# Latents' attention of a hybrid diffusion step: raw scores are moved out of the PSUM banks by ScalarE in thirds, maxima and shifts work on the moved copy, and value products run two pairs behind

## The reference

```python
def one_block(qblk):
    s = jnp.einsum('bqkgd,blkd->bkgql', qblk, k).astype(jnp.float32) * scale
    p = jax.nn.softmax(s, axis=-1).astype(v.dtype)
    return jnp.einsum('bkgql,blkd->bqkgd', p, v)
```

## Time and profile before

| what | us |
|---|---|
| median of 3 runs | 2715.31 |
| lowest and highest | 2712.28, 2717.53 |
| the profiled execution, its own time | 2714.14 |
| its span in the profile | 2712.3 |
| first scores of the latents to the last output copy of their attention | 326.99 to 701.76 |

### The profile page before, as it was taken

How to read it: one execution, slowest core, us unless ns; L and a number is a source line. 1 busy time by engine, 2 the same in 40 slices (tenths; PEclk the granted TensorE clock), 3 DMA queues, 4 the chain that set the end, 5 groups by cost and what they waited for, 6 DMA issues and landing times.

```text
span 2712.3 us, 37077 instructions
## 1 busy us (share of the span) xinstructions
PE 2565.8 (95%) x15039; PEld 1926.0 (71%) x15039; DVE 1645.7 (61%) x2459; ACT 1193.8 (44%) x1950; POOL 235.9 (9%) x259
## 2 busy tenths in 40 slices
PE   7999799999899999999999999997799999999994
PEld 3444499999788677575767888884577777777773
DVE  2555677777333345757566344556676776777774
ACT  3311334444333233434343333342576766666663
POOL 1111100000000000000001000000010110101012
PEclk8999899999899999999999999998899999999997
DMA  9310000000101200101012200525688897988887
GB/s 320 135 66 32 0 1 1 1 1 1 63 32 51 96 16 1 55 1 55 1 39 82 78 32 32 190 98 186 236 289 309 281 329 271 312 305 289 305 274 221
DMA packets 176603, 345.01 MB, mean 127 GB/s; under 512 B 9338, under 2 KB 37580, under 8 KB 176434
## 3 DMA queue, kind: packets, MB, share of 16 engines
q1 hardware_dynamic: 166396, 314.09, 32.6%
q0 software_dynamic: 9472, 28.32, 4.1%
q10 hardware_dynamic: 566, 0.24, 0.0%
HBM read 304.35 MB, written 38.27 MB: 126 GB/s over the span
## 4 chain that ended last, share of the span: by engine, by line
PE 63%; issue 22%; DMA 8%; DVE 5%; ACT 1%; POOL 0%; POOLq 0%; DVEq 0%; SPq 0%; ACTq 0%
PE ps L1004 16%; PE ps L228 8%; DMA ffn_scratch<-WK 6%; PE ps L1358 6%; PE ps L751 5%; PE ps L1310 5%; PE ps L779 4%; PE ps L1905 4%; DVE WK L848 2%; PE ps L1421 2%; PE ps L1404 1%; PE ps L1324 1%; PE ps L2448 1%; PE ps L1381 1%; PE ps L1931 1%
## 5 line engine op out<-in xcount | busy, mean ns | idle before, releaser
L2527 ACT ACTIVATE RWr<-R 128x1024 fp32r<-128x1024 f32 x384 | 377.8, 1055 | 71.9 <-PE ps L2448 69.3
L2622 DVE TENSOR_TENSOR W_low<-R,RWr 128x1024 fp32r<-128x1024 f32 x256 | 301.4, 1219 | 84.5 <-ACT RWr L2527 82.4
L2448 PE MATMUL ps<-RWr,R1r 128*128 128x512 f32 x1024 | 329.6, 396 | 6.0 <-DVE R1r L2610 4.3
L1004 PE MATMUL ps<-W_high,tile_high 128*128 128x512 f32 x640 | 251.2, 392 | 7.7 <-DVE W_low L1082 7.2
L1004 PE MATMUL ps<-W_low,tile_high 128*128 128x512 f32 x640 | 250.6, 392 | 0.0
L1004 PE MATMUL ps<-W_high,tile_low 128*128 128x512 f32 x640 | 250.5, 391 | 0.0
L228 PE MATMUL ps<-RW,R 128*128 128x512 f32 (+1 forms) x640 | 248.9, 542 | 0.0
L2448 PEld LDWEIGHTS ps<-RWr,R1r 128*128 128x128 f32 x1024 | 192.9, 188 | 58.2 <-issue 14.2
L228 PEld LDWEIGHTS ps<-RW,R 128*128 128x128 f32 x640 | 119.2, 191 | 105.4 <-issue 101.5
L1074 DVE TENSOR_TENSOR tile_low<-R,tile_high 128x1024 fp32r<-128x1024 f32 x80 | 97.9, 1223 | 156.9 <-ACT tile_high L1030 156.7
L2622 DVE TENSOR_TENSOR tile_high<-R,RWr 128x1024 fp32r<-128x1024 f32 x128 | 150.8, 1219 | 29.8 <-ACT RWr L2527 29.5
(11 more groups left out here) (346 smaller groups left out, 4638.1 us busy)
## 6 DMA issues: line engine op xcount, KB each, us to landing
R<-in_w_dram SPq DMA_DIRECT2D x96, 2048.0 KB, 13.3
RW<-in_w_in_dram SPq DMA_DIRECT2D x11, 1024.0 KB, 5.4
R<-in_w_mod_dram SPq DMA_DIRECT2D x5, 2048.0 KB, 12.8
RW<-in_w_in_dram SPq DMA_DIRECT2D x5, 2048.0 KB, 8.4
RW<-in_w_mod_dram SPq DMA_DIRECT2D x4, 2048.0 KB, 11.3
WK<-in_w_mod_dram SPq DMA_DIRECT2D x3, 2048.0 KB, 7.8
mix_scratch<-R SPq DMA_DIRECT2D x10, 512.0 KB, 2.6
R<-mix_scratch SPq DMA_DIRECT2D x10, 512.0 KB, 7.0
```

Of the source, the lines that this page charges most:

```text
L1004: i = pe.matmul(bank(m % 4), Tsplit[a][:, m % 2, k, :], Wsplit[b][:, k, :], start=(k == 0 and n == 0), stop=(k == KD - 1 and n == 2))
L2448: m = pe.matmul(bank(bank_of(e, i, j)), stat[a][:, k, :], w[b][:, k % 2, :], start=(k == 0 and z == 0), stop=(k == KD - 1 and z == 2))
L2527: act.activation(ring_high[n % RING], pair_raw[i][j][:, 2 * q:2 * q + 2, :], ACT.Copy).then_inc(S("weights_high"), 1)
L2622: dve.tensor_tensor(ring_low[n % RING], pair_raw[i][j][:, 2 * q:2 * q + 2, :], ring_high[n % RING].bitcast(F32), ALU.subtract).then_inc(S( ...
```

## The change

The raw scores leave PSUM by a plain copy. `keep_scores(u)` (ScalarE) copies banks 0 to 5 in three pieces of 1024 elements into `probs[u % 3]`, which now has three buffers in place of two (the third lies in the front of WK; the small tiles of the stage move to where the rotary tables lay). `scores_done` rises three times a turn, once for each third; `scores(u + 1)` waits for `scores_kept` in place of the shifted pieces. `top_of` reads the copy in SBUF, by thirds: three maxima over 4 blocks each and two of two tiles. `shift` reads the copy and adds in place. `shifts` has two buffers. The value products run two turns behind the scores. The diff, with the moved tile addresses left out:

```diff
-            def scores(u, half):
+            def scores(u):
...
                     if u and b % 4 == 0:
-                        pe.wait_ge(S("kept_by_dve"), CTX_K + 3 * (u - 1) + b // 4 + 1)
+                        pe.wait_ge(S("scores_kept"), 3 * (u - 1) + b // 4 + 1)
...
-                m.then_inc(S("scores_done"), 1)
+                    if b % 4 == 3:
+                        m.then_inc(S("scores_done"), 1)
...
-            for u in range(len(turns) + 2):
-                if u < len(turns):
-                    scores(u, 0)
-                    scores(u, 1)
-                if u >= 2:
-                    turn_rows(u - 2)
-                v = u - 1
-                if 0 <= v < len(turns):
-                    weigh_rows(v, 0, range(0, 8))
-                if u < len(turns):
+            N = len(turns)
+            for u in range(N + 3):
+                if u < N:
+                    scores(u)
+                v = u - 2
+                if 0 <= v < N:
+                    weigh_rows(v, 0, range(0, 10))
+                if u >= 3:
+                    turn_rows(u - 3)
+                if 0 <= v < N:
+                    weigh_rows(v, 0, range(10, 12))
+                    weigh_rows(v, 1, range(0, 4))
+                if u < N:
                     turn_max(u)
-                if 0 <= v < len(turns):
-                    weigh_rows(v, 0, range(8, 12))
-                    weigh_rows(v, 1, range(0, 3))
-                if u < len(turns):
+                if 0 <= v < N:
+                    weigh_rows(v, 1, range(4, 12))
+                if u < N:
                     spread_max(u)
-                if 0 <= v < len(turns):
-                    weigh_rows(v, 1, range(3, 12))
...
-            def top_of(u, half):
-                dve.wait_ge(S("scores_done"), CTX_K + 2 * u + half + 1)
-                o = half * 3 * BANK
-                ch(dve.tensor_reduce(top_halves[half], ps[:, o:o + 3 * BANK].rearrange("p (b n) -> p n b", n=2 * P), AX, ALU.max))
-                if half:
-                    dve.tensor_tensor(top_halves[1], top_halves[0], top_halves[1], ALU.max).then_inc(S("max_ready"), 1)
+            def top_of(u, third):
+                dve.wait_ge(S("scores_kept"), 3 * u + third + 1)
+                src = probs[u % 3][:, 4 * third:4 * third + 4, :].rearrange("p b n -> p n b")
+                ch(dve.tensor_reduce(tops[min(third, 1)], src, AX, ALU.max))
+                if third == 1:
+                    ch(dve.tensor_tensor(tops[0], tops[0], tops[1], ALU.max))
+                elif third == 2:
+                    dve.tensor_tensor(tops[1], tops[0], tops[1], ALU.max).then_inc(S("max_ready"), 1)
...
-            def shift(u):
-                dve.wait_ge(S("max_kept"), u + 1)
-                dve.wait_ge(S("values_weighed"), CTX_Q + max(0, u - 1))
-                for p_ in range(3):
-                    dve.tensor_tensor(pT[u % 2][:, 4 * p_:4 * p_ + 4, :], ps[:, p_ * 2 * BANK:(p_ + 1) * 2 * BANK].rearrange("p (b n) -> p b n", b=4),
-                                      shifts.unsqueeze(1).broadcast_to([P, 4, 2 * P]), ALU.add).then_inc(S("kept_by_dve"), 1)
+            def shift(u, p_):
+                if p_ == 0:
+                    dve.wait_ge(S("max_kept"), u + 1)
+                E = probs[u % 3][:, 4 * p_:4 * p_ + 4, :]
+                dve.tensor_tensor(E, E, shifts[u % 2].unsqueeze(1).broadcast_to([P, 4, 2 * P]), ALU.add).then_inc(S("kept_by_dve"), 1)
...
-            for u in range(len(turns) + 1):
-                if u < len(turns):
-                    top_of(u, 0)
-                    top_of(u, 1)
+            N = len(turns)
+            for u in range(N + 2):
+                if 1 <= u <= N:
+                    shift(u - 1, 0)
+                    shift(u - 1, 1)
+                if u < N:
+                    for third in range(3):
+                        top_of(u, third)
+                if 1 <= u <= N:
+                    shift(u - 1, 2)
+                if u < N:
                     negate(u)
-                    shift(u)
-                if u:
-                    invert(u - 1)
+                if u >= 2:
+                    invert(u - 2)
...
+            def keep_scores(u):
+                act.wait_ge(S("values_weighed"), CTX_Q + max(0, u - 2))
+                if u == 2:
+                    act.wait_ge(S("kept_by_dve"), CTX_K)
+                for third in range(3):
+                    act.wait_ge(S("scores_done"), CTX_K + 3 * u + third + 1)
+                    act.activation(probs[u % 3][:, 4 * third:4 * third + 4, :],
+                                   ps[:, third * 2 * BANK:(third + 1) * 2 * BANK].rearrange("p (b n) -> p b n", b=4), ACT.Copy).then_inc(S("scores_kept"), 1)
...
-            for u in range(len(turns) + 2):
-                if u >= 2:
-                    keep_columns(u - 2)
-                if u < len(turns):
-                    if u:
-                        act.wait_ge(S("kept_by_dve"), CTX_K + 3 * u)
-                    keep_max(u)
-                    for p_ in range(3):
-                        exps_of(u, p_)
-                if 1 <= u <= len(turns):
-                    keep_rows(u - 1)
-                    T, g, hp = turns[u - 1]
+            N = len(turns)
+            for u in range(N + 3):
+                if u < N:
+                    keep_scores(u)
+                if u >= 3:
+                    keep_columns(u - 3)
+                if 1 <= u <= N:
+                    for p_ in range(3):
+                        exps_of(u - 1, p_)
+                if u < N:
+                    keep_max(u)
+                if 2 <= u < N + 2:
+                    keep_rows(u - 2)
+                if u < N:
+                    T, g, hp = turns[u]
```

More of the change, by code:

```diff
@@ L246, in build_program @@
         vv = work(14 * HKV * VW).rearrange("p (b n) -> p b n", b=14)
+        cos_at = used[0]
         cos_t = work(T_LAT * 64).rearrange("p (t f) -> p t f", t=T_LAT)
@@ L659, in build_program @@
         turns = [(T, g, hp) for T in range(T_CTX, NT) for g in range(HKV) for hp in range(2)]
[L660 to L664, removed]
+        probs = pT + [WK[:, 0:12 * 2 * P].rearrange("p (b n) -> p b n", b=12)]
+        assert cos_at + 2048 <= WORK_N
+        out_rows, tops, shifts = [[WK[:, cos_at + (2 * i + n) * 2 * P:cos_at + (2 * i + n + 1) * 2 * P] for n in range(2)] for i in range(3)]
+        top_diag = WK[:, cos_at + 1536:cos_at + 1792].rearrange("p (a n) -> p a n", a=2)
+        minus = WK[:, cos_at + 1792:cos_at + 1792 + P]
         def sset(s):
@@ L682, in queries_read @@
             else:
-                eng.wait_ge(S("scores_done"), CTX_K + 2 * (turns.index((T, g, 1)) + 1))
+                eng.wait_ge(S("scores_done"), CTX_K + 3 * (turns.index((T, g, 1)) + 1))
         def tile_scores(pe, T, k):
@@ L736, in pe_attn @@
                 weigh(T_CTX - 1, 3, b)
-            def scores(u, half):
+            def scores(u):
                 T, g, hp = turns[u]
[L741 to L747, removed]
+                if hp == 0:
+                    pe.wait_ge(S(f"queries_staged{g}"), T + 1)
+                if u == 0:
+                    pe.wait_ge(S("kept_by_act"), CTX_K)
+                    pe.wait_ge(S("kept_by_dve"), CTX_K)
+                for b in range(NK_LAT):
                     if u and b % 4 == 0:
-                        pe.wait_ge(S("kept_by_dve"), CTX_K + 3 * (u - 1) + b // 4 + 1)
+                        pe.wait_ge(S("scores_kept"), 3 * (u - 1) + b // 4 + 1)
                     for n, (a, c_) in enumerate(((0, 0), (0, 1), (1, 0))):
@@ L785, in turn_rows @@
                 pe.wait_ge(S("kept_by_act"), CTX_K + u + 1)
-                pe.wait_ge(S("kept_by_dve"), CTX_K + 3 * min(u + 2, len(turns)))
+                pe.wait_ge(S("max_kept"), min(u + 3, len(turns)))
                 for a in range(2):
@@ L920, in keep_columns @@
                 act.activation(R2[:, o:o + 2 * P], ps[:, 6 * BANK + 2 * P:7 * BANK], ACT.Copy).then_inc(S("attn_kept"), 1)
+            def keep_scores(u):
[6 more added lines that the diff above has]
+                                   ps[:, third * 2 * BANK:(third + 1) * 2 * BANK].rearrange("p (b n) -> p b n", b=4), ACT.Copy).then_inc(S("scores_kept"), 1)
             def keep_max(u):
                 act.wait_ge(S("max_spread"), u + 2)
-                act.activation(shifts, bank(6, 2 * P), ACT.Copy).then_inc(S("max_kept"), 1)
+                if u >= 2:
+                    act.wait_ge(S("kept_by_dve"), CTX_K + 3 * (u - 1))
+                act.activation(shifts[u % 2], bank(6, 2 * P), ACT.Copy).then_inc(S("max_kept"), 1)
             def exps_of(u, p_):
                 act.wait_ge(S("kept_by_dve"), CTX_K + 3 * u + p_ + 1)
-                E = pT[u % 2][:, 4 * p_:4 * p_ + 4, :]
+                E = probs[u % 3][:, 4 * p_:4 * p_ + 4, :]
                 act.activation(E, E, ACT.Exp, scale=SCALE).then_inc(S("probs_ready"), 1)
```

11 lines of the change are left out of this document (5 added, 6 removed).

## The result

The change makes the kernel slower: a median of 2755.04 us (2753.47 to 2756.17, 4 runs) against 2716.36 us of before in the same comparison, a ratio of 1.0145 with a 95% interval of 1.0127 to 1.0162. The forecast was 2699.4 us, range 2694 to 2710. The profiled execution has a span of 2754.3 us.

What follows compares the result with a forecast made beforehand. The prediction took TensorE as the bound, with one stall per turn waiting for VectorE's maxima. Turns -18.0, fill -1.4 and drain +3.5 summed to -15.9 us, from 2715.31 to 2699.4 us, range 2694 to 2710.

Steps and rivals of the forecast that it cites:

- turns of 10.62: Steady turns 2 to 31: each falls from 11.22 to 10.62 us, saving 18.0 us over 30 turns.
- The stall of 0.65: TensorE's transposes of the maxima start 0.65 us late each turn, waiting for VectorE; removing this saves 0.60 a turn.
- TensorE's own idle of 0.37: Steady turns: the lower bound on time removed per turn, 0.37 us, from TensorE's own idle; 0.60 was taken instead.
- The step that failed: VectorE's reduction of 1024 elements from the SBUF copy, priced between two measured rows at 1.22 us.
- The overlap margin: VectorE in a steady turn: maxima ready 0.5 us before TensorE asks, third shift piece and `negate` done 0.4 before.
- the ring's own sum: Steady turn's cycle from spreading through `keep_max`, shifts, maxima and `negate` to spreading: 10.25 us against TensorE's 10.62.
- slow strides: Rival: strided SBUF reductions cost 1.05 us more each, the turn becomes 13.4, time near 2784 us; chance 0.06.
- point of decision: VectorE's reductions: the change turns from gain to loss if each takes over 0.32 us more than priced.
- The drain's 1.1 for a lowered clock: Drain after the last turn: 1.1 us (0 to 3.5) added to 16.6 for TensorE's lowered clock, giving 17.7.
- The fill's sum, 22.6: Up to the scores of turn 2: 20.7 us plus 1.9 for the lower clock, 22.6 against 24.05 before.
- ScalarE's margin: ScalarE's exps end by 10.8 and `keep_max` can start at 10.92: 0.1 us to spare, the thinnest margin.

Runs made afterwards that it cites:

- e1: The changed kernel with each of the three reductions reading the same 1024 elements as runs of four neighbours, so maxima of other groups: 2698.38 us, ratio 0.9941.
- e2: The changed kernel with the reductions reading the PSUM banks by thirds, same 1 KB step, all else kept: 2699.93 us, ratio 0.9940; repeated with more rounds, 2698.60 us.
- e11: The changed kernel with pairwise contiguous maxima, all shifts first, one product instruction moved, ScalarE's next-queries copy between second and third exp: 2700.12 us, ratio 0.9944.
- e8: The kernel before with only TensorE's order changed: 11, 6 and 7 value products around the transposes in place of 8, 7 and 9: 2711.35 us, ratio 0.9988.
- e7: The changed kernel with one reduction left at the 1 KB step and two reading the copy contiguously: 2709.68 us, ratio 0.9981, turn 10.94 us.
- e4: The kernel before plus a stretch behind its last turn timing VectorE operations alone at several steps: lone SBUF reduction with the 1 KB step 1.88 us.

## Why the prediction was wrong

**The bound of before** was read rightly, and so was the gain from leaving it. The forecast said turns of 10.62 once nothing waits; e1, e2 and e11 have 10.57, so 19.6 us in place of 18.0. The stall of 0.65 counted start to start was the right reading, and TensorE's own idle of 0.37 the wrong one. What the forecast did not say is that the old turn was a ring through the scores (e8): leaving it took the whole structure, not the cover.

**The step that failed** is one term: "The reduction of 1024 elements has no row ... so 0.686 + 512 x 1.05 = 1.22". The two rows it stood between were a contiguous read of SBUF and a strided read of PSUM; the operation is a strided read of SBUF, and neither bounds it. It takes 1.96, 0.74 more. The overlap margin built on it (0.4 to 0.5 us to spare on VectorE's ring) went with it, and TensorE waited in every turn. With the measured price in the ring's own sum, 10.25 + 3 x 0.74 = 12.47, against a measured 12.38. All other durations were within 0.01 of their rows: moves 1.026, shift pieces 1.218, exps 1.05. The margins were there as well: in e7 the ring works out as 10.94 - 0.74 = 10.20, forecast 10.25.

**The rival that came true** is the second, slow strides, with the right mechanism and the right ring, at a price of 1.05 that was 0.74: 2784 forecast, 2755 measured. Its point of decision, 0.32 more per reduction, was passed by more than twice. It had 0.06. The trace of before neither bore it out nor spoke against it: eight elements would be only 0.006 us longer at 0.74 us per 1024, and the PSUM row with the same step was taken for evidence about SBUF. A named rule on one side, a row of the wrong memory on the other and no row of the right one are worth more than 0.06. A chance near a half would have been fair, and a range up to 2784 with it.

**Fill and drain.** Cut as in the forecast (first score load, scores of turn 2, end of the last turn, end of the stage), e2, which is the forecast's kernel without the slow step, has 22.7, 317.4 and 16.2 where before has 24.4, 336.6 and 14.2: -1.7, -19.2 and +2.0, forecast -1.4, -18.0 and +3.5. The drain's 1.1 for a lowered clock did not come (granted clock 1.00 from 669.6 to 685.0, where before had 0.76). The fill's sum, 22.6, met the measured 22.7 partly by luck. Its chain without the clock ended at 20.7, 2.0 short, and the forecast added 1.9 for the lower clock at the scores of turn 2. In e2 the granted clock was 0.50 from 337.2 to 344.0 us, that is in the scores of turn 1, whose loads run from 338.55 to 345.46 (6.9 us, where a steady turn has 4.35). So the stage is 18.9 shorter in e2, forecast 15.9. In the changed kernel the first shift of turn 1 also comes 3 us later than in e2, where the six reductions of turns 0 and 1, 0.74 longer each, have little beside them.

The account of the +38.6 us of stage in the changed kernel, cut at `keep_max` of turns 1 and 31: fill 22.5 to 26.4, +3.9; turns 336.8 to 371.5, +34.7; drain 15.8 both times.

**ScalarE's margin**, called the thinnest, did not bind: e1 leaves `keep_max` an idle 0.56 ahead of it each turn.

## What to carry to other kernels

A duration is bound to the memory and the access pattern it was measured with: before work is moved from PSUM to SBUF, look at the innermost step of each operand, and where no row has that pair, measure it alone first, as e4 does in one run. When an operation of VectorE has two operands in SBUF, look at what POOL runs beside it. And when one stall is to be removed, draw the ring that it lies on; the ring tells which changes can help (the change, e1 and e2 differ in one line, and the change lies 55 to 57 us above the other two).

## What the hardware showed that was not expected

- VectorE's reductions read fp32 from SBUF with an inner step of 16 bytes or more at 1.88 to 2.02 us per 1024 elements, against 1.22 at 8 bytes or less and 1.22 from PSUM at 1 KB. A plain copy goes from 0.69 to 1.14. Steps of 16 bytes and 1 KB cost nearly the same (1.96 and 1.88).
- A VectorE operation with two SBUF operands and a POOL operation on SBUF did not run side by side. The one that comes second waits: POOL 2.23 in place of 1.27, or the shift 0.77 to 1.09 longer. In the kernel before POOL's operation took 1.27 throughout, but it never met the shift: it ran beside a reduction from PSUM (POOL from 366.69, the reduction from 366.76 at its usual 1.76). So no run shows whether a shift with one operand in PSUM would have been held.
- The granted clock stayed at 1.00 through a drain with TensorE's pauses of 1.53, 1.25 and 1.25 us (e2 and the change). Before, it was at the lower level (0.50) from 689.9 to 696.7 us, behind one pause of 3.98 that began at 687.6:

```profile
691.62 0.29 PEld L789 LDWEIGHTS ps<-ident,WK 128*128 128x128 f32 x2 [3.98 <-ACT WK L936]
```
